# Expert stage of a streaming encoder on one core: the V table as streamed blocks for four tiles, by-token gathers for the other five

## What is computed

```python
s1 = einsum('thd,hkd->thk', q[:, :, 0], sub_keys[0]); s2 = einsum(..., sub_keys[1])   # 128 keys each
v1, i1 = top_k(s1, 16); v2, i2 = top_k(s2, 16)
best, sel = top_k(v1[..., :, None] + v2[..., None, :], 16)      # over 256 sums
idx = take(i1 * 128 + i2, sel); gate = softmax(best)            # 16384 experts
ug = u_tab[idx]; vg = v_tab[idx]                                # rows of 1024 floats
act = gelu(einsum('td,thkd->thk', h2, ug))
y = einsum('thk,thkd->td', gate * act, vg)
x = x + gate2 * rms(y)
```

## Time and profile before

| | |
|---|---|
| median of 3 runs | 3820.19 us |
| span of the profiled execution | 4199.6 us |
| TensorE busy | 3314.8 us (79%) |
| VectorE busy | 2313.6 us (55%) |
| GpSimd busy | 2152.0 us (51%) |
| ACT busy | 950.0 us (23%) |
| HBM read | 1220 MB |

### The profile page before, as it was taken

The page is one execution under the profiler, slowest core; times in us unless marked ns, Lnnn a source line. Parts: engine busy times, 40 slices in busy tenths (PEclk is TensorE's granted clock), DMA queues, the critical chain, the costliest instruction groups (busy, mean ns, idle before and its releaser), DMA issues.

```text
span 4199.6 us, 38180 instructions
## 1 busy us (share of the span) xinstructions
PE 3314.8 (79%) x9348; PEld 1593.5 (38%) x9348; DVE 2313.6 (55%) x5821; ACT 950.0 (23%) x2161; POOL 2152.0 (51%) x2222
## 2 busy tenths in 40 slices
PE   8998989928777777877777777777777777887677
PEld 2454555513333333333333333333333333333222
DVE  2104552867755665555665655566555665556442
ACT  1003773312221221112112211211121121112111
POOL 0000300236566665666666666566666665666665
PEclk9999999969898898898888888888888888888888
DMA  9104102159999999999999999899999999999997
GB/s 357 64 15 126 32 19 113 61 188 352 344 357 359 353 359 354 347 368 343 341 359 347 350 356 344 332 354 355 360 347 358 358 357 348 343 363 358 361 362 303
DMA packets 365168, 1245.51 MB, mean 297 GB/s; under 512 B 52129, under 2 KB 57505, under 8 KB 362751
## 3 DMA queue, kind: packets, MB, share of 16 engines
q0 software_dynamic: 313504, 1141.02, 72.4%
q1 hardware_dynamic: 48852, 96.77, 6.6%
q10 hardware_dynamic: 2576, 5.10, 0.4%
HBM read 1220.34 MB, written 22.39 MB: 296 GB/s over the span
## 4 chain that ended last, share of the span: by engine, by line
PE 38%; issue 17%; another core or an unknown queue 9%; DVE 5%; DMA 4%; POOL 3%; ACT 1%; DVEq 0%; POOLq 0%; ACTq 0%; SPq 0%
PE ps_y L1692 33%; PE ps_q L950 5%; DMA urow<-in_u_tab,idx 3%; POOL urow L1473 2%; POOL vrow L1473 1%; DMA vrow<-in_v_tab,idx 1%; DVE urow L1612 1%; ACT diag L1580 1%; DVE aux L993 0%; PE ps_s L961 0%; DVE i L996 0%; DVE sel L996 0%; DVE i L992 0%; DVE aux L1029 0%
## 5 line engine op out<-in xcount | busy, mean ns | idle before, releaser
L1692 PE MATMUL ps_y<-vrow,diag 128*128 128x512 f32 (+1 forms) x4352 | 2220.8, 665 | 647.5 <-issue 329.9
L1612 DVE CUSTOM_DVE_ANT_0 urow<-urow,ps_h 128x1024 f32<-128x1024 f32 x1088 | 1299.8, 1220 | 1025.2 <-DMA urow<-in_u_tab,idx 865.6
L1692 PEld LDWEIGHTS ps_y<-vrow,diag 128*128 128x128 f32 (+1 forms) x4352 | 884.3, 209 | 1893.6 <-issue 1576.9
L1473 POOL DMA_INDIRECT vrow<-in_v_tab,idx x1088 | 1031.6, 948 | 785.7 <-issue 287.4
L1473 POOL DMA_INDIRECT urow<-in_u_tab,idx x1088 | 1030.7, 947 | 430.5 <-issue 282.8
L1580 ACT ACTIVATE diag<-const,wgt 128x128 f32<-128x128 f32 x1024 | 373.1, 396 | 1766.2 <-PE ps_y L1692 643.3
L950 PE MATMUL ps_q<-aux,w_q_sb 128*128 128x128 f32 x2048 | 271.7, 292 | 58.1 <-issue 49.4
L950 PEld LDWEIGHTS ps_q<-aux,w_q_sb 128*128 128x128 f32 x2048 | 263.9, 207 | 94.4 <-issue 93.2
L1293 POOL TENSOR_TENSOR xo<-xo,ot 128x1024 f32<-128x1024 f32 (+1 forms) x9 | 21.1, 2343 | 352.2 <-DVE ot L1249 352.2
L530 PE MATMUL ps_z<-hT,w_in_sb 128*128 128x512 f32 (+1 forms) x576 | 190.5, 491 | 4.6 <-DVE hT L448 4.6
L625 POOL MEMSET kTs<- 128x384 f32 x1 | 0.4, 418 | 322.7 <-POOLq L344 322.7
(11 more groups left out here) (181 smaller groups left out, 2341.3 us busy)
## 6 DMA issues: line engine op xcount, KB each, us to landing
ada<-in_w_ada SPq DMA_DIRECT2D x12, 2048.0 KB, 12.5
urow<-in_u_tab,idx POOLq DMA_INDIRECT x1088
vrow<-in_v_tab,idx POOLq DMA_INDIRECT x1088
w_in_sb<-in_w_in SPq DMA_DIRECT2D x8, 1024.0 KB, 17.9
w_q_sb<-in_w_query SPq DMA_DIRECT2D x8, 1024.0 KB, 14.3
x<-in_x_p ACTq DMA_DIRECT2D x8, 512.0 KB, 6.6
w_out_sb<-in_w_out SPq DMA_DIRECT2D x8, 512.0 KB, 7.0
xo<-in_x_p SPq DMA_DIRECT2D x8, 512.0 KB, 3.7
```

The source lines that it names most:

```text
L1473: nc.gpsimd.indirect_dma_start(ring[k % RING][:, :], None, A[table][:, :], bass.IndirectOffsetOnAxis(ap=places[:, col:col + 1], axis=0)).t ...
L1612: nc.vector.tensor_tensor_reduce(out=urow[k % RING][:, :], in0=urow[k % RING][:, :], in1=ps_h[:, :], scale=1.0, scalar=0.0, op0=ALU.mult, ...
L1692: last = nc.tensor.matmul(ps_y[0:rows, c], diag[s % DIAGS][:, 0:rows], vrow[k % RING][:, c], start=(s == 0), stop=(s == PH * width(n) - 1))
```

## The change

The order of v work is no longer by slot. Tiles 2, 3 and 5, 6 (`PAIRS`) are *dense*: for each pair SP streams the V table once, in 128 blocks of 128 rows, and TensorE multiplies each block by a matrix `G` of both tiles (128 rows of the block by 128 tokens, four 128x512 products a block). `G` holds each token's weights at its experts' places, and is made of one-hots: for four tokens (a group) VectorE makes the one-hot of the row index times the weight (`one_hot_i`), ACT the one-hot of the column index (`one_hot_j`: four Abs, one Relu), TensorE multiplies them, and ACT copies the result into `G`. For tiles 0, 1, 4, 7, 8 v rows are gathered by token: a token's 128 rows lie on 128 partitions, and its weights are one column of a 128x32 stationary that is zero elsewhere, so that a product adds one output row of a strip of 32 rows. Items are ordered so that neighbouring ones belong to different strips. An *item* is a token or a block; `DUE` says how many items are placed by which slot, `BURST` at which slots the groups stand. 268 of the 832 items stand behind the last slot.

The queries of all prompt tokens are made in the first 16 units, 512 tokens at a time; scores go through DRAM (`s_d`) and come back a head at a time. The search is cut into 16 steps (`Find.step`), one behind each product (two in tile 0). The loop over tiles is written out, with waits on constants. The rings are 5 u and 6 v buffers instead of 8 and 8, and `w_q`'s place later holds one `G`.

```diff
+PAIRS = ((2, 3), (5, 6))
+    tokens(0); tokens(1); blocks(0); tokens(4); blocks(1); tokens(7); tokens(8)
+    DUE = [(0, 0), (72, 0), (192, 64), (200, 64), (456, 192), (526, 192), (716, 320), (746, 320), (852, 448), (908, 448),
+           (NU, 564)]
+    BURST = {2: (330, 3), 3: (459, 2), 5: (748, 2), 6: (838, 2)}
 SP:
+            for v, (n, p, c) in enumerate(ITEMS):
+                if n is None:
+                    sp.wait_ge(v_used, v - RV + 1)
+                    sp.dma_start(vrow[v % RV][:, :], A["v_tab"][c * NKEY:(c + 1) * NKEY, :])\
+                        .then_inc(block_full[v % RV], 16)
 GpSimd:
-                            gather("v_tab", vrow, v_full, n, h, k)
+                    gather_u(s, n, width(n) * h + k)
+                    for v in items(s):
+                        if ITEMS[v][0] is not None:
+                            gather_v(v)
 VectorE:
-                        products(un, uh)
-                        find.search(own, dve, dve_passed, n + 1, h - 1)
-                        weights(un, uh)
+                for k in range(width(n)):
+                    dve.wait_ge(u_full[s % RU], 16 * (s // RU + 1))
+                    nc.vector.tensor_tensor_reduce(out=urow[s % RU][:, :], in0=urow[s % RU][:, :], in1=ps_h[:, :],
...
+                    if k == 1 and q:
+                        weights(q - 1)
+                        for i in ([k] if n else [2 * k, 2 * k + 1]):
+                            find.step(own, dve, tn, th, i, sc[j % 2], ...)
+                    if behind is not None and 3 <= k <= 5:
+                        find.normalise(own, dve, *UNITS[behind], k - 3)
+                    if group(s):
+                        one_hot_i(*group(s))
+                    if s in FINISH:
+                        finish(FINISH[s])
 ACT:
-                        weight = wgt[h % 2][:, k:k + 1]
-                            nc.scalar.activation(diag[s % DIAGS][:, :], ident, ACT.Copy, scale=weight)\
+                for u in range(GT):
+                    own.add(nc.scalar.activation(oneB[u], iota[:, :], ACT.Abs, bias=T[:, 1, t:t + 1]))
+                own.wait()
+                nc.scalar.activation(flat[:, HALF:2 * HALF], flat[:, HALF:2 * HALF], ACT.Relu, bias=1.0, scale=-1.0)\
+                    .then_inc(b_ready, 1)
...
+                nc.scalar.activation(W[:, :, 31], src, ACT.Copy).then_inc(W_ready, 1)
 TensorE:
-                    last = nc.tensor.matmul(ps_y[0:rows, c], diag[s % DIAGS][:, 0:rows], vrow[k % RING][:, c],
+                    for x in range(2):
+                        for half in range(2):
+                            last = nc.tensor.matmul(ps_y[x][:, f], G[x][:, b, :], vrow[v % RV][:, f], start=(b == 0),
+                                                    stop=(b == NKEY - 1))
+                else:
...
+                    r = slice(32 * b, 32 * (b + 1))
+                    for half in range(2):
+                        last = nc.tensor.matmul(sums(n)[r, f], W[:, b, 31 - a:63 - a], vrow[v % RV][:, f],
+                                                start=(a == 0), stop=(a == 31), skip_group_check=True)
+            for q, (n, h) in enumerate(UNITS):
+                if q < 2 * PH:
+                    queries(q, 0)
+                    if q:
+                        scores(q - 1)
+                    queries(q, 1)
```

More of the change, by code:

```diff
@@ new lines, in experts, with tokens, blocks @@
+    idx_ready, s_read = find.idx_ready, find.s_read
+    RU, RV, RW = 5, 6, 3
+    NGRP, GT, HALF = P // 4, 4, 4 * P
+    NU = first(NT + 1)
+    LAST = len(UNITS) - 1
+    dense = [n for pair in PAIRS for n in pair]
+    unit = {u: q for q, u in enumerate(UNITS)}
+    ITEMS, begin, end = [], {}, {}
+    def tokens(n):
+        begin[n] = len(ITEMS)
+        quads = 4 if n else 2
+        ITEMS.extend((n, g, a) for g in range(32) for a in range(quads))
+        end[n] = len(ITEMS)
+    def blocks(p):
+        for n in PAIRS[p]:
+            begin[n], end[n] = len(ITEMS), len(ITEMS) + NKEY
+        ITEMS.extend((None, p, c) for c in range(NKEY))
@@ new lines, in _ @@
+            take_w(NT)
+            for v in items(NU):
+                if ITEMS[v][0] is not None:
+                    put_w(v)
+                if v == end[5] + 5:
+                    norm(5)
+                    store(5)
+                elif v == end[5] + 9:
+                    norm(6)
+                    store(6)
+                elif v == end[7] + 5:
+                    norm(7)
+                    store(7)
+            norm(8)
+            store(8)
+            act.wait_ge(y_out, 16 * (NT + 1))
@@ new lines, in queries @@
+            def queries(z, side):
+                r, h = divmod(z, PH)
+                if z:
+                    pe.wait_ge(q_copied, 2 * z + side - 1)
+                c = 2 * h + side
+                for k in range(KC):
+                    last = nc.tensor.matmul(ps_y[1][:, HALF * side:HALF * (side + 1)], w_q[:, k, c * P:(c + 1) * P],
+                                            h2T[:, k, HALF * r:HALF * (r + 1)], start=(k == 0), stop=(k == KC - 1))
+                last.then_inc(q_mm, 1)
@@ new lines, in _ @@
+            nc.tensor.matmul(ps_g[:, 0:NKEY], nones, mask, start=True, stop=True).then_inc(iota_mm, 1)
+            pe.wait_ge(iota_done, 1)
+            for t in range(NT):
+                transposes(t)
+            pe.wait_ge(hT_copied, 2 * NT)
+            for q, (n, h) in enumerate(UNITS):
+                if q < 2 * PH:
+                    queries(q, 0)
+                    if q:
+                        scores(q - 1)
+                    queries(q, 1)
+                elif q == 2 * PH:
+                    scores(q - 1)
+                for k in range(width(n)):
+                    s = slot(n, h, k)
+                    if s in T_SLOT:
+                        turn(*T_SLOT[s])
+                    if group(s):
+                        make_group(*group(s))
+                    for v in items(s):
+                        add_item(v)
@@ L1714, in constants @@
+            turn(NT, "w")
+            for v in items(NU):
+                add_item(v)
 def constants():
```

950 lines of the change are left out of this document (593 added, 357 removed).

## The result

| | before | after |
|---|---|---|
| median | 3820.26 us (3820.03 to 3822.70, 4 runs) | 3767.39 us (3757.58 to 3771.45, 4 runs) |
| ratio | 1 | 0.9856 (95%: 0.9842 to 0.9871) |
| span of a profiled execution | 4199.6 us; again: 3816.7 us | 3762.7 us |
| HBM read | 1220 MB | 1100 MB |

The changed kernel is 1.4% faster. The prediction said 3878 us and slower with a chance of 0.61: the direction was wrong, the range held the time. The sum's own range, 3800 to 3950, did not hold it.

The account below looks back on a forecast made before the run. Gather transfers were taken to bind the kernel before; after the change, each stretch at its slowest resource summed to 2974 us against 2916, 58 slower: 3878 us. The range was 3715 to 3990, the sum's own 3800 to 3950.

Parts of the forecast that it names:

- Step 11: Last 256 gathers: between 1.31 us each (transfers) and 1.745 (products one behind the other), the middle 1.53 taken: 391 us.
- rival (a): Last 256 items: products on different strips run side by side, 1.31 us an item, tail 335, 3822 us, no change; chance 0.23.
- step 2: Slots 16 to 64: VectorE binds, six heads of 20.3 us, 122 us; slots 64 to 72 add 15.
- step 3: Slots 72 to 200: transfers 265, TensorE 246, VectorE 239 us; engines this close cost each other something: 275 us.
- step 4: Slots 200 to 456, v of tile 1: transfers 508, VectorE 504, GpSimd 476 us; 525 taken.
- step 5: Slots 456 to 526: VectorE slots 131, one-hots 26, rest of tile 1 about 11: 168 us.
- step 12: The end, 11 us as before, and four tile starts where VectorE waits 3 us each for gelu and copies, 12 us.
- The two block steps: Blocks for tiles 2, 3 (slots 526 to 746) and 5, 6: TensorE 447 us each; the first stretch 485 with its finishes.
- Step 1: First gather to slot 16: h2 tiles, queries, copies, then the gelu VectorE waits for at slot 9; 65 us.
- rival (b): The profile's stretch lies on all engines, not on the transfers: 3722 us, faster; chance 0.17.
- Rival (c): Blocks: TensorE's clock stays mixed, 4.07 us a block, block stretches grow by 148, 4026 us; chance 0.15.
- three signs of being wrong: DMA share above 0.95 throughout, a start of 30 us instead of 65, or blocks further apart than 3.6 us.

Follow-up runs that it names:

- run 4: The changed kernel with all items of tiles 7 and 8 written to one strip of 32 output rows instead of four; 3846.97 us.
- run 6: The changed kernel with two u buffers added to the six v buffers for the last 256 items; 3739.98 us.
- run 5: The changed kernel with VectorE's u products over 512 of the 1024 columns, transfers unchanged; 3748.04 us, one time.
- run 2: The kernel before with its hardware loop over tiles 2 to 7 written out, nothing else; 3803.02 us.
- run 3: The kernel before with the loop written out and its search cut into 16 steps between products, V rows still gathered by slot; 3785.68 us.
- run 1: The kernel before, unedited, profiled once more; 3818.77 us, profiled span 3816.7 us.
- run 7: The changed kernel with a different start, tile 4's items spread over slots 746 to 892, and eight buffers for the last 256 items; 3707.82 us.
- run 9: The changed kernel with eight buffers for the last 256 items, and items of tile 4 (to slot 892) and tile 1 (to 508) spread; start unchanged; 3677.88 us.
- run 8: The kernel with three edits (start, tile 4, ring of eight), and prompt queries over 4 of 8 row blocks only; 3685.11 us, one time.
- run 10: The kernel with tiles 1 and 4 spread and eight buffers, plus a new start: ACT's gelu and score loads ahead of query copies; 3675.38 us.

## Why the prediction was wrong, step by step

The sum, us from the first gather, as predicted and as the trace of the changed kernel has it:

| step | predicted | measured |
|---|---|---|
| 1, to slot 16 | 65 | 64.2 |
| 2, slots 16 to 64, and to 72 | 137 | 125.8 |
| 3, slots 72 to 200 | 275 | 270.6 |
| 4, slots 200 to 456 | 525 | 515.3 |
| 5, slots 456 to 526 | 168 | 160.9 |
| 6, slots 526 to 746 | 485 | 473.2 |
| 7, slots 746 to 852 | 313 | 308.1 |
| 8, slots 852 to 908 | 136 | 130.3 |
| 9 and 10, blocks and handover | 456 | 443.9 |
| 11, the last 256 items | 391 | 358 |
| 12, the end; four tile starts | 11 and 12 | 10.5; the starts lie in the steps above |
| sum | 2974 | 2861 |

Against 2916 for before (a number that held: 1.31 us a transfer and pauses), the forecast was 58 us slower and the measurement 55 faster. The 113 us between have two parts.

- **Step 11, "I take the middle, 1.53", failed by 33 us.** The overlap that rival (a) asks for was there (run 4), and where data lay ready there was more of it: 0.89 us an item, against its 1.31. What held the tail at 1.40 an item was a ring of six buffers (run 6), which neither the step nor rival (a) priced. Rival (a)'s 3822 us was 335 for the tail in the same sum; the measured 358 lies between the two, and with eight buffers it is 335.3.
- **The surcharges on the other steps failed by 80 us, all in one direction, and this decided the sign.** With step 11 right and the rest as it stood the sum would be 2941, still slower; with step 11 as it stood and the rest right, 2894, faster. Steps 2 to 5, 7, 8 and 12 took their slowest resource and then 4 to 17 us for engines "this close" to each other, or for starts, stops and remainders; they make 55 of the 80. They came out at about their slowest resource: step 4 at 515 for 508 of transfers, step 3 at 271 for 265. (In step 2 the change between the two kinds of work was added at 1.2 us a head of 8 slots, where 0.1 a slot makes 0.8.) The two block steps make 24: the blocks of a pair took 443 us instead of 447 and began 2 and 7 us ahead of slots 526 and 908. The four tile starts of step 12 were priced at 3 us each; VectorE's waits for `ps_h`, to which they belong, come to 6.8 us in the whole run.
- **Some steps had the right size and the wrong reason.** Step 1 was 64 us as predicted, and that was luck: the gelu was not what held VectorE first. Its order of time in the changed kernel shows a wait of 36.7 us for the gain rows, whose load SP issues behind the eight h2 tiles, and one of 11.6 us for the turn of tile 0's indices behind the first queries:

```profile
930.51 1.21 DVE L1874 TENSOR_TENSOR io<-io,G 2x1024 f32<-2x1024 f32 x1 [36.73 <-DMA io<-mod_d]
...
949.07 0.23 DVE L1844 CAST idxT<-ps_g 128x64 uint32<-128x64 f32 x1 [11.64 <-PE ps_g L1970]
```

  Steps 2, 5 and 8 were given to VectorE; run 5 shows that taking 26, 37 and 30 us of its work out of them shortens them by 6, 5 and 4 us. By the trace, the query units and the one-hot rounds stand right behind it there.
- **The price of what went away was put at nothing.** Register steps inside the searches were given no price, and the search as one piece was not mentioned. Runs 2 and 3 show 17 and then 17 us: with the search in one piece the queue ran down. The prediction had the number for this, 1.31 to 1.34 against 1.28 us a transfer. It is no term of the 113 us, though: in the changed kernel the stretches bound by transfers took 1.31 to 1.34 us each (308.1 / 236, 515.3 / 388, 270.6 / 202), about what the sum had.
- **The profiled execution.** The 4199.6 us were taken for the program's; run 1 shows that they were one execution's. The sum for the runs did not use them, but rival (b) with 0.17 did. Only rival (b) had a faster kernel at its centre, and the range reached down to 3715 for its sake; that the range held the time is luck. One of the two arguments against (b), that a record's 0.436 repeats to the hundredth, does not hold in its own rows: the earlier trace rows has 16.29 us for 32, which is 0.509. Rival (c), 0.15, fell too: 0.430 us a record in the blocks, clock 1.00.
- **The signs.** The counts, the blocks without a gap and 1.40 us an item came as the prediction said for being right; the span near 4090 and a low share in the last 300 us of the blocks (1.03 until u ended) did not. None of its three signs of being wrong came, and the direction was wrong all the same.

Where the expected gain of streaming went is settled for the most part: into stretches without v items or without u slots, and into the ring of six. Runs 6, 7 and 9 filled three of them, and 3767 became 3678 us, which is 108 us below the one kernel without streaming that had the search spread (run 3). What keeps the first 64 slots at 172 to 180 us is shown only in part (runs 8 and 10).

## What to carry to other kernels

Fewer transfers pay only where the queue still has something to do. Write down the DMA share of every stretch after such a change and move work into the ones that fall short. Before believing a profile that is longer than the runs, take it again. And if a sum of stretches is within a few per cent of the old time, small allowances all on one side decide its sign: give them both signs, or none.

## What the runs showed of the hardware that was not expected

- Gathers of 128 rows of 4 KB ran at 405 to 406 GB/s for 2000 us on end when 16 buffers kept the queue full (run 3), at 407 to 409 with eight (run 6), and at 380 with six (the tail).
- Products of 32 output rows on four strips overlap: where data lay ready the pace was 0.221 us a record, in the tail, where the rows came no faster, 0.338, and on one strip 0.432 (run 4).
- TensorE's granted clock was 0.52 in slots 456 to 526 (nearly all at 1.2 GHz) with one-hot groups alone, and 0.82, a mix of both levels, with v items between them (run 9); this stretch became shorter although TensorE had more to do. In slots 852 to 908 the clock rose alike, from 0.54 to 0.82, and the stretch became longer.
